# Recurrent mixer on TensorE: two dense pieces and then two recurrent steps, in place of one and one

## The chip, the cores and the metric

The kernel runs on one core of one Trainium2 chip. The metric is the device time of one execution in microseconds (us). TensorE is called PE, VectorE DVE, ScalarE ACT, GpSimd POOL, and SyncE SP.

## The reference, cut to what matters

A decoder block over 1024 tokens of width 1024. One large projection feeds two token mixers; what concerns the change is the recurrent one, with four heads of 128 keys and 128 values:

```python
proj = jnp.einsum('bsd,dn->bsn', h, w_in[i])
f = lb + (1.0 - lb) * jax.nn.sigmoid(f_lin)          # decay, per key and token
log_f, k, v, q = jnp.log(f), 1.0 - f, i_lin, jax.nn.silu(q_lin)
# S_t = diag(f_t) S_{t-1} + k_t v_t^T ;  o_t = S_t^T q_t, computed in chunks of tokens:
scores = jnp.einsum('bhtk,bhtsk,bhsk->bhts', q_c, decay, k_c)
o = einsum(scores, v_c) + einsum(q_c * exp(b), state)
new_state = exp(b_last) * state + einsum(k_c * exp(b_last - b), v_c)
o = o * lax.rsqrt(mean(o*o) + RMS_EPS) * norm_g * jax.nn.silu(og_lin)
```

Afterwards come a softmax mixer with eight heads, the merge of both, a squared-ReLU MLP, an embedding gate and two layer norms. The change touches none of these.

## The kernel before

**Dense work.** Weights are split into a high and a low part and each product is made of three matmul passes. A dense job is one 128-row block of the projection for all 1024 tokens. It has eight pieces, one for each 128 of the contraction; `feature_job` yields after each. A piece (`three_pass`, L774, L776, L778) is six matmuls of 128x512. A job writes one of two PSUM sets in turn, and before its first piece `begin` waits until the job before the last (same set) has been read, and until POOL has split its weights. At a job's end the semaphore `mm_done` lets ACT or DVE read it, and lets POOL convert (L683) and split (L686) the next weight chunk into the freed pages.

**Recurrent work.** Each head has 24 steps (`hg_step(n, i)`), which are called here:

- kt0, kt1 (i = 0, 1): transposes of the decayed keys, L864
- level 0 to level 15 (i = 2 to 17): two halves of the tokens at eight levels of the recursion over a 128-token chunk, 4 matmuls each, L882. Even levels are the first half of the tokens, odd ones the second.
- u0, u1 (i = 18, 19): state updates, L891
- o0, o1 (i = 20, 21): outputs, L901 and L904
- r0, r1 (i = 22, 23): means of squares, L909

These are plain float32 matmuls, and the profile records each as two. In each iteration of its own loop DVE forms the decay differences of a level (`level_sub`, L1721, L1722), multiplies those of the level before (`level_mul`, L1730, L1731) after ACT has taken their exponential (L1272), and merges the level before that by one more into the scores (`level_take`, L1737). Level i waits for the take of level i - 2 and for its own multiplications. Between them DVE has further work once in each head: `gate_part` (L1711) right behind take 0, L1781 behind take 2, `q_part` (L1681) behind take 6, `f_part` (L1686 to L1688) behind take 12, `decay_part` (L1695, L1701) behind take 14, and the states (L1748, L1750) and `kd_part` (L1706) behind take 15. u1 waits for take 15. At the end of a head ACT computes a logarithm (L1314) and an exponential (L1315) for r0 and then for r1, and DVE writes the head's output (`head_out`, L1761, L1762) for each before it begins the next head.

**The order on PE.** `dense_stream` gives 112 pieces of 14 jobs. Twelve pieces run first, then each recurrent step stands behind one piece (108 pieces, 96 steps), then four pieces are left. Jobs begin at pieces 0, 8, 16 and so on. In each head one job begins right behind level 1; it uses the PSUM set that `gate_part` must have read first. It is called the gated job here.

Of the kernel before, what the change touches and what calls it, by code (L numbers as in the profile page):

```python
# [27 lines left out]
NHG = 4  # L28
# [114 lines left out]
HG_LEAD = 12  # L143
# [67 lines left out]
def block_kernel(nc, x, p, ln0_g, ln0_b, w_in, hg_lb, hg_norm_g, fox_fb, w_a, w_b, w_o, ln1_g, ln1_b,  # L211
                 w_ff1, w_ff2, w_pg, w_p, ln2_g, ln2_b, c_ident, c_causal, c_masks,
                 h_scratch, c_scratch, pw_scratch, acc_scratch, act_scratch, out):
    with ExitStack() as ctx:
# [19 lines left out]
        def F(page, off=0, n=1024):  # L234
            t, at = f32_pages[page + off // 1024]
            return t[:, at + off % 1024:at + off % 1024 + n]
# [168 lines left out]
        def vtile(page, t):  # L405

            return F(page + t // 2, (t % 2) * HG, HG)
# [360 lines left out]
        def _(pe):  # L768
# [87 lines left out]
            def hg_step(n, i):  # L856
                par = n % 2
                if i < 2:

                    pe.wait_ge(kd_ready, n + 1)  # L860
                    if n:
                        pe.wait_ge(rs_ready, 2 * (n - 1) + i + 1)
                    for c in range(4 * i, 4 * i + 4):
                        ins = nc.tensor.transpose(bankM[i][:, (c % 4) * P:(c % 4 + 1) * P],  # L864
                                                  F(PG_T2, c * P, P), ident[:, :])
                    ins.then_inc(kt_turned, 1)
                elif i < 18:
                    hl = i - 2
                    lv, hf = hl // 2, hl % 2
                    if lv < LEVELS - 1:  # L870
                        pe.wait_ge(ab_ready, 14 * n + hl + 1)
                        base = PG_AB + (hl % 4) // 2
                        lhs = rhs = F(base, (hl % 2) * HALF, HALF)
                    else:
                        pe.wait_ge(q_ready, n + 1)
                        lhs, rhs = F(PG_HK + par, hf * HALF, HALF), F(PG_HQ + par, hf * HALF, HALF)
                    if lv == 0:
                        pe.wait_ge(kt_done, 2 * n + hf + 1)
                    else:
                        pe.wait_ge(pred_done, 16 * n + hl - 1)  # L880
                    for c in range(4):
                        ins = mm(bankM[hf][:, c * P:(c + 1) * P], lhs[:, c * P:(c + 1) * P],  # L882
                                 rhs[:, c * P:(c + 1) * P], start=True, stop=True)
                    ins.then_inc(lvl_done, 1)
                elif i < 20:
                    u = i - 18
                    pe.wait_ge(pred_done, 16 * n + 14 + u + 1)
                    pe.wait_ge(kt_done, 2 * n + u + 1)
                    pe.wait_ge(v_ready, TT)
                    for c in range(4 * u, min(4 * u + 4, TT - 1)):  # L890
                        ins = mm(bankM[u][:, (c % 4) * P:(c % 4 + 1) * P], F(PG_KT, c * P, P),  # L891
                                 vtile(PG_VHG, c)[:, n * P:(n + 1) * P], start=True, stop=True)
                    ins.then_inc(upd_done, 1)
                elif i < 22:
                    hf = i - 20
                    pe.wait_ge(st_ready, 2 * n + hf + 1)
                    pe.wait_ge(qe_ready, n + 1)
                    pe.wait_ge(pred_done, 16 * n + 16)
                    for c in range(4 * hf, 4 * hf + 4):
                        o = bankM[2 + hf][:, (c % 4) * P:(c % 4 + 1) * P]  # L900
                        ins = mm(o, vtile(PG_VHG, c)[:, n * P:(n + 1) * P], F(PG_S, c * P, P),  # L901
                                 start=True, stop=c == 0)
                        if c:
                            ins = mm(o, F(PG_ST, c * P, P), F(PG_T1, c * P, P), start=False, stop=True)  # L904
                    ins.then_inc(o_done, 1)
                else:
                    hf = i - 22
                    pe.wait_ge(sq_done, 2 * n + hf + 1)
                    mm(bankM[hf], mean_w[:, :], F(PG_T3, hf * HALF, HALF), start=True,  # L909
                       stop=True).then_inc(rms_done, 1)  # L910

            def dense_stream(names):
                for name in names:
                    yield from std(name)

            stream = dense_stream([("g", 0), ("q", 1), ("f", 1), ("g", 1), ("q", 2), ("f", 2), ("g", 2),
                                   ("q", 3), ("f", 3), ("g", 3), ("fq", 0), ("fk", 0), ("gx", 0), ("crow",)])
            for step in range(HG_LEAD + 24 * NHG):
                next(stream)
                if step >= HG_LEAD:  # L920
                    hg_step(*divmod(step - HG_LEAD, 24))
            for _ in stream:
                pass
            for t in range(TT):
# [43 lines left out]
            def turn_outputs(n):  # L968
                pe.wait_ge(o_ready, 16 * (n + 1))
                pe.wait_ge(x_ready, min(16 * (n + 1) + 2, 64))  # L970
                for i in range(TT):
# [4 lines left out]
            stream = dense_stream([(x, n) for n in range(1, NPAIR) for x in ("fq", "fk")]  # L976
                                  + [("gx", i) for i in range(1, 16)])
# [1216 lines left out]
```

## Time and profile before

| | |
|---|---|
| time, median of 3 runs | 1777.24 us (1775.79 to 1780.26) |
| time of the profiled execution | 1777.77 us |
| span of the profiled execution | 1775.8 us |
| PE busy | 1697.9 us, 96% of the span |
| DVE busy | 1028.1 us, 58% |
| mean granted clock of PE | 0.992 of full speed |
| recurrent mixer, first kt0 to last r1 | 117.3 to 352.4 us of the span |

Busy time is summed over the instructions of an engine. A wait is the idle time of an engine before an instruction, with the instruction that released it. "PEclk" is the granted clock of PE: 1.00 is 2.4 GHz and 0.50 is 1.2 GHz.

### The profile page before, as it was taken

The page shows a single profiled execution, that of the slowest core. Times are in us where ns is not written, and L with a number is a line of the kernel's source. Part 1 is how long each engine was busy: PE and PEld are TensorE (multiplying, and loading weights), DVE is VectorE, ACT ScalarE, POOL GpSimd, SP SyncE. Part 2 cuts the span into 40 slices and gives each one's busy share as a digit, 9 for nine tenths or more (in the row PEclk, how much of TensorE's full clock was granted, in tenths as well). Part 3 has the DMA queues.
Part 4 walks back from the last instruction along what each step waited for, and adds up shares of the span by engine and source line. Part 5 has one row for each costly group of instructions (what it writes and reads, how often), then busy time and mean ns, then how long its engine had stood idle before and what let it go on. Part 6 is the DMA issues. An engine that isn't in the chain of part 4 may idle for free.

```text
span 1775.8 us, 21568 instructions
## 1 busy us (share of the span) xinstructions
PE 1697.9 (96%) x8304; PEld 1381.6 (78%) x8304; DVE 1028.1 (58%) x1560; ACT 622.0 (35%) x954; POOL 623.6 (35%) x438
## 2 busy tenths in 40 slices
PE   4999999999999999999999998999999999999997
PEld 3888877886677678887878776788888887888886
DVE  7557987612222230003641676998766668866987
ACT  2143443213333333002012354244545453343341
POOL 3221121403011002333444438766665523342334
PEclk9999999999999999999999998999999999999999
DMA  8210000111001001111133343545443489778672
GB/s 275 71 48 25 24 25 25 47 48 48 25 25 48 25 12 37 48 48 36 52 103 109 129 155 108 174 150 209 163 163 131 148 275 306 227 224 238 196 228 95
DMA packets 207924, 200.80 MB, mean 113 GB/s; under 512 B 8520, under 2 KB 178760, under 8 KB 205776
## 3 DMA queue, kind: packets, MB, share of 16 engines
q1 hardware_dynamic: 204656, 188.35, 33.9%
q10 hardware_dynamic: 3168, 11.08, 1.6%
q8 instruction: 67, 1.10, 0.3%
q14 instruction: 33, 0.27, 0.1%
HBM read 153.23 MB, written 46.17 MB: 112 GB/s over the span
## 4 chain that ended last, share of the span: by engine, by line
PE 84%; DVE 9%; DMA 2%; SPq 2%; issue 1%; ACT 1%; POOL 1%; DVEq 0%; ACTq 0%; POOLq 0%
PE dense L774 10%; PE dense L776 10%; PE dense L778 10%; PE dense L964 3%; PE dense L1057 3%; PE dense L1059 3%; PE dense L1058 3%; PE dense L1137 3%; PE dense L1139 3%; PE dense L1138 3%; PE mixA L945 2%; PE mixA L943 2%; PE mixB L955 2%; PE dense L827 2%; PE dense L829 2%; PE dense L828 2%
## 5 line engine op out<-in xcount | busy, mean ns | idle before, releaser
L774 PE MATMUL dense<-parts 128*128 128x512 f32 x880 | 302.2, 413 | 7.5 <-DVE parts L1840 2.6
L683 POOL CAST parts<-page 128x1024 fp32r<-128x1024 f32 x55 | 61.3, 1114 | 681.9 <-PE dense L778 561.6
L776 PE MATMUL dense<-parts 128*128 128x512 f32 x880 | 284.9, 393 | 0.0
L778 PE MATMUL dense<-parts 128*128 128x512 f32 x880 | 283.8, 392 | 0.0
L686 POOL TENSOR_TENSOR parts<-page,parts 128x512 fp32r<-128x512 f32 x134 | 190.8, 1444 | 49.2 <-ACT parts L1406 44.8
L778 PEld LDWEIGHTS dense<-parts 128*128 128x128 f32 x880 | 166.1, 189 | 36.6
L776 PEld LDWEIGHTS dense<-parts 128*128 128x128 f32 x880 | 166.2, 189 | 35.7
L774 PEld LDWEIGHTS dense<-parts 128*128 128x128 f32 x880 | 154.6, 191 | 34.9 <-issue 9.2
L748 POOL TENSOR_TENSOR parts<-page,parts 128x512 fp32r<-128x512 f32 x52 | 89.8, 1749 | 208.8 <-ACT parts L1517 208.8
L1818 DVE CUSTOM_DVE_ANT_0 page<-mixA,page 128x128 f32<-128x128 f32 (+3 forms) x64 | 48.5, 758 | 190.0 <-PE mixA L946 190.0
L723 POOL TENSOR_TENSOR page<-page 128x512 f32<-128x512 f32 x80 | 123.1, 1538 | 59.4 <-PE dense L1059 26.4
L731 POOL TENSOR_TENSOR parts<-page,parts 128x512 fp32r<-128x512 f32 x80 | 113.4, 1419 | 61.7 <-ACT parts L1453 57.0
L1057 PE MATMUL dense<-parts 128*128 128x512 f32 x288 | 112.5, 391 | 0.3 <-issue 0.3
L1059 PE MATMUL dense<-parts 128*128 128x512 f32 x288 | 112.2, 390 | 0.0
L1058 PE MATMUL dense<-parts 128*128 128x512 f32 x288 | 112.1, 389 | 0.0
L1527 ACT CAST parts<-page 128x1024 fp32r<-128x1024 f32 x56 | 58.6, 1052 | 144.6 <-DVE page L2053 123.2
L1350 ACT ACTIVATE page<-page,nmx 128x128 f32<-128x128 f32 (+3 forms) x64 | 49.7, 777 | 166.0 <-DVE nmx L1823 166.0
L1453 ACT CAST parts<-page 128x512 fp32r<-128x512 f32 x132 | 78.2, 614 | 67.6 <-POOL page L723 62.7
L1840 DVE TENSOR_TENSOR parts<-page,parts 128x1024 fp32r<-128x1024 f32 x8 | 11.4, 1486 | 140.4 <-ACT parts L1366 140.4
L1137 PE MATMUL dense<-parts 128*128 128x512 f32 x224 | 87.4, 390 | 3.6 <-DVE parts L1978 3.6
L1138 PE MATMUL dense<-parts 128*128 128x512 f32 x224 | 87.2, 389 | 0.0
L1139 PE MATMUL dense<-parts 128*128 128x512 f32 x224 | 87.2, 389 | 0.0
(230 smaller groups left out, 3611.4 us busy)
## 6 DMA issues: line engine op xcount, KB each, us to landing
page<-in_w_ff SPq DMA_DIRECT2D x104, 512.0 KB, 5.9
page<-act_scratch SPq DMA_DIRECT2D x56, 512.0 KB, 5.8
page<-in_w_in SPq DMA_DIRECT2D x90, 256.0 KB, 3.4
act_scratch<-page SPq DMA_DIRECT2D x16, 1024.0 KB, 3.9
act_scratch<-page SPq DMA_DIRECT2D x16, 768.0 KB, 7.0
page<-in_w_o SPq DMA_DIRECT2D x32, 256.0 KB, 3.2
h_scratch<-page ACTq DMA_DIRECT2D x8, 512.0 KB, 2.8
page<-c_scratch SPq DMA_DIRECT2D x8, 512.0 KB, 4.2
```

What stands on the lines that cost most here:

```text
L686: ins = nc.gpsimd.tensor_tensor(R(lo, at, HALF), F(RAW + c % 2, at, HALF), R(hi, at, HALF).bitcast(F32), ALU.subtract)
L723: PT(raw(i), a, b, op).then_inc(s_sum, 1)
L731: PT(slot_half(q, i, True), F(SLOT[i], HALF, HALF), slot_half(q, i, False).bitcast(F32), ALU.subtract).then_inc(sum_split, 1)
L774: mm(o, whi, x_, start=first, stop=False)
L776: mm(o, whi, x_, start=False, stop=False)
L778: ins = mm(o, wlo, x_, start=False, stop=last)
L1057: mm(o, hi, x_part(i, k, False), start=k == 0, stop=False)
L1058: mm(o, hi, x_part(i, k, True), start=False, stop=False)
L1059: ins = mm(o, lo, x_part(i, k, False), start=False, stop=k == 3)
L1137: mm(o[:, cols], hi, xh, start=j == 0, stop=False)
L1138: mm(o[:, cols], hi, xl, start=False, stop=False)
L1139: ins = mm(o[:, cols], lo, xh, start=False, stop=j == 7)
```

## The change

The loop advances by two: two pieces are issued, then two steps. Odd steps keep their place among the pieces; each even step (kt0, the even levels, u0, o0, r0) goes behind one more piece and stands right before its odd neighbour. The count of pieces and steps is the same, and no other engine's program changes.

```diff
-            for step in range(HG_LEAD + 24 * NHG):
-                next(stream)
+            for step in range(0, HG_LEAD + 24 * NHG, 2):
+                for _ in range(2):
+                    next(stream)
                 if step >= HG_LEAD:
-                    hg_step(*divmod(step - HG_LEAD, 24))
+                    for s in (step, step + 1):
+                        hg_step(*divmod(s - HG_LEAD, 24))
```

## Rows read from the trace of the kernel before

**Rows 1.** Two windows: PE, PEld, DVE, ACT, POOL busy; PEclk, DMA, GB/s.
```profile
290.00:320.00 30.00, 26.54 (x143) 22.05 (x142) 27.92 (x53) 12.82 (x20) 8.86 (x6) 0.94 0.13 36
...
300.00:305.00 5.00, 4.99 (x23) 4.58 (x24) 5.00 (x13) 2.10 (x3) 0.71 (x1) 0.66 0.42 108
```
**Rows 2.** Waits in 98 to 362: us in total, times, longest.
```profile
PE mixA L882 <- DVE page L1737: 6.4, 8, 1.4
```
**Rows 3.** Timeline of PE (start, duration, line, shape, count): pieces and steps undisturbed.
```profile
109.10 0.61 PE L774 MATMUL dense<-parts 128*128 128x512 f32 x2
...
110.46 0.61 PE L774 MATMUL dense<-parts 128*128 128x512 f32 x2
...
195.07 1.05 PE L882 MATMUL mixA<-page 128*128 128x128 f32 x8
195.88 0.71 PE L774 MATMUL dense<-parts 128*128 128x512 f32 x2
...
197.35 1.05 PE L882 MATMUL mixA<-page 128*128 128x128 f32 x8
...
226.75 0.38 PE L901 MATMUL mixB<-page 128*128 128x128 f32 x2
...
228.46 0.70 PE L774 MATMUL dense<-parts 128*128 128x512 f32 x2
```
**Rows 4.** Timeline of PE: r1 of the first head; levels 0, 1 and gated job of the second.
```profile
173.30 1.02 PE L909 MATMUL mixA<-page,mean_w 128*128 128x512 f32 x2
...
179.41 1.16 PE L882 MATMUL mixA<-page 128*128 128x128 f32 x8
...
181.79 1.05 PE L882 MATMUL mixA<-page 128*128 128x128 f32 x8
183.94 0.70 PE L774 MATMUL dense<-parts 128*128 128x512 f32 x2 [1.10 <-DVE page L1711]
```
**Rows 5.** Timeline of DVE there: output for r1, first level_sub, take 0, gate.
```profile
175.75 0.69 DVE L1761 TENSOR_TENSOR page<-mixB,page 128x512 f32<-128x512 f32 x1 [0.31 <-ACT page L1315]
...
177.14 0.42 DVE L1721 TENSOR_TENSOR page<-page 128x256 f32<-128x256 f32 x1
...
181.96 0.73 DVE L1737 COPY_PREDICATED page<-masks,mixA 128x512 f32<-128x512 uint8 x1
182.58 1.21 DVE L1711 TENSOR_TENSOR page<-dense,page 128x1024 f32<-128x1024 f32 x1
```
**Rows 6.** Timeline of ACT there: logarithm and exponential for r1, and the next instruction.
```profile
174.36 0.69 ACT L1314 ACTIVATE page<-mixA,eps 128x512 f32<-128x512 f32 x1 [0.50 <-PE mixA L909]
175.08 0.63 ACT L1315 ACTIVATE page<-page 128x512 f32<-128x512 f32 x1
175.62 1.04 ACT L1226 ACTIVATE page<-page 128x1024 f32<-128x1024 f32 x1
```
**Rows 7.** Timelines of DVE (takes 14 and 15) and PE (u1), second head.
```profile
215.99 0.73 DVE L1737 COPY_PREDICATED page<-masks,mixA 128x512 f32<-128x512 uint8 x1 [1.03 <-PE mixA L882]
...
220.41 0.74 DVE L1737 COPY_PREDICATED page<-masks,mixA 128x512 f32<-128x512 uint8 x1
...
221.74 0.83 PE L891 MATMUL mixA<-page 128*128 128x128 f32 x6
```
**Rows 8.** First head: DVE's take 0 and a level_sub, POOL's split of a chunk.
```profile
122.01 0.73 DVE L1737 COPY_PREDICATED page<-masks,mixA 128x512 f32<-128x512 uint8 x1 [0.37 <-PE mixA L882]
...
124.72 1.50 DVE L1722 TENSOR_TENSOR page<-page 128x256 f32<-128x256 f32 x1
...
124.60 2.78 POOL L686 TENSOR_TENSOR parts<-page,parts 128x512 fp32r<-128x512 f32 x2
```
**Rows 9.** Timeline of POOL, fourth head: a chunk's conversion.
```profile
295.83 1.04 POOL L683 CAST parts<-page 128x1024 fp32r<-128x1024 f32 x1 [30.38 <-PE mixA L864]
```
**Rows 10.** Timeline of PE: two long stalls of the run.
```profile
300.01 2.08 PE L882 MATMUL mixA<-page 128*128 128x128 f32 x8 [2.91 <-DVE page L1731]
...
1065.62 1.06 PE L1030 MATMUL mixB<-ident,page 128*128 128x128 f32 x8 [2.52 <-issue]
```

## Prediction

> **What bounds the kernel now.** I read the page first. PE is the busy engine through nearly the whole span, as its table shows, so only PE's own work and PE's waiting count. Then the waits between 98 and 362 us, where the mixer runs: the largest of PE's is for DVE's takes, 6.4 us in 8 waits [rows 2]. The windows say why: from 290 to 320 PE was busy for 26.54 us of 30 and DVE for 27.92 [rows 1]. The reader is to see a balance of two engines. Last I read the timelines of PE, DVE, ACT and POOL over each head, since only the order of instructions changes, and no sum can show that. They show one pattern in each head: from its output work to take 11 DVE runs without a pause and PE waits for it; behind take 11 it is the other way round, and DVE waits for PE's levels.
>
> **The price of a switch.** The plain reason for such a change would be that PE loses time whenever it goes from one kind of matmul to the other. A piece alone takes 110.46 - 109.10 = 1.36 us. A level and a piece take 197.35 - 195.07 = 2.28, so a level standing alone costs 0.92. What does it cost right behind another step? Eight records run 195.88 - 195.07 = 0.81 us up to the next dense matmul, sixteen (o1) run 228.46 - 226.75 = 1.71: the eight more cost 0.90 [rows 3]. So a pair saves 0.02 us, and 48 pairs 1.0 us. From below the bound is nothing. From above it is the piece behind a step, 2.28 - 0.81 = 1.47 us against 1.36 alone: were all 0.11 us saved 48 times, that would be 5.3 us. I take 1.0, since a step gets 0.09 us back at its entry that a second one behind it can't get again.
>
> **What moves.** Odd steps stay where they are among the pieces, even ones come one piece, 1.36 us, later. The way from take i - 2 to level i keeps its two pieces and one step, and deadlines of even steps get later, which is harmless. What counts is what DVE or ACT begins when an even step is done and an odd step or a piece waits for. I went through a head with that question and found three places. At takes 2 to 10 the even level is still done before DVE comes to it (at take 6 by about 0.2 us, the least), and I cost them at nothing; if that cover is gone, a take starts some tenths later.
>
> Place one, level 0 to the gated job. Take 0 and the gate need 183.94 - 181.96 = 1.98 us up to the gated piece. In the second head level 0 now starts at about 180.57, at the end of two undisturbed pieces, and is done at 181.7; take 0 was at 181.96 anyway, as DVE was late [rows 4, 5]. So nothing is added, and the third head repeats this within 0.1 us. In the first head take 0 did wait for level 0, 0.37 us [rows 8], and now starts 1.36 us later, at 123.37.
>
> Place two, take 14 to u1. Take 14 waited 1.03 us for level 14; from its start to that of take 15, with the decay scans between, are 220.41 - 215.99 = 4.42 us. Level 14 comes 1.34 us later, take 15 starts near 221.75 and ends near 222.5, and u1, which started at 221.74, waits until about 222.65 [rows 7]. With some hundredths for a step behind a stall that is 0.95 us in each of the three heads that prepare a next one. The fourth has no decay work and loses nothing. Queued behind the waiting u1 are two pieces, o0, o1, two pieces, r0 and r1, so the whole next head is late by as much.
>
> Place three, r0 and r1. They now follow each other by 0.87 us in place of 2.24. ACT needs 0.72 us from r0's logarithm to its exponential and 0.54 from there to the next instruction. r1's logarithm started 174.36 - 173.30 = 1.06 us behind r1; now r0's starts at 0.17 and r1's at 1.43 [rows 4, 6]. DVE's output for r1 started 175.75 - 173.30 = 2.45 us behind r1 [rows 4, 5]; now that for r0 is only done at 2.96. So DVE starts the next head 0.5 us later, three times, and since it has no pause from there to take 11, PE gets this in full at level 11.
>
> **POOL against DVE.** A level_sub instruction of 0.42 us [rows 5] took 1.50 while POOL split a weight chunk, and POOL's two halves last 2.78 us [rows 8], so each such event costs DVE up to three caught instructions, about 0.6, 1.1 and 1.1 us. Takes and the gate keep their 0.73 and 1.21 us. A job's last piece now stands ahead of an even step, so POOL is set off about 0.9 us earlier. In the first head that is a gain: DVE waits for level 0 while POOL converts, take and gate cover the first half of the split, and one instruction is caught in place of three. With 1.36 for the late take 0 and 1.1 - 2.8 for the caught ones, take 1 comes 0.3 us earlier. In the second and third heads I take the meeting as before less 0.15 us, since POOL gets in when DVE reaches take 0. In the fourth a chunk moves from levels 1 to 3 to the time of the gate, which saves about 0.7.
> The Trainium skill (SBUF — State Buffer, Who interferes with whom) gives the reason: an instruction with two SBUF inputs and a GpSimd instruction that reads SBUF block each other for a whole instruction, and the order of issue decides which waits; one with at most one SBUF input stays out of it. The trace agrees, with 1.50 us for the one and 1.21 for the other. By the order of issue the meeting could also fall worse than I take it, which is rival B.
>
> **Sum without the clock.** First head: -0.3 at level 11, +0.95 for u1, +0.6. Second and third: 0.5 - 0.15 + 0.95 = +1.3 each. Fourth: 0.5 - 0.15 - 0.7 = -0.35, and -0.05 for a short wait that goes, -0.4. Together +2.8 us. The 1.0 us of the switches I don't subtract again: where DVE sets the pace it is worth nothing, and behind take 11 it is within the roundings of these positions.
>
> **The clock.** PE now issues two pieces and both levels ahead of the gated job and then has nothing. Its idle time there grows from 1.3 us to 2.2 in the second and third heads and comes to about 2.2 in the fourth, whose stall of 2.91 ahead of level 0 shrinks to about 1.5. Behind those 2.91 us eight records took 2.08 us for 1.05, behind 2.52 us they took 1.06 [rows 10]; the granted clock was 0.66 over 300 to 305 [rows 1], so part of it at the lower level of 1.2 GHz, and (1 - 0.66) x 5 = 1.7 us of work was lost. Of the six stalls of 1.8 to 2.9 us in the run before, three were followed by such a stretch. Behind the gated piece PE has only 0.3 us of slack to DVE, and DVE then waits for levels in turn, so I put 1.1 us of the 1.7 on the path. Half a chance at three places: +1.6 us, from 0 to 5.1. The sum is +4.4. It is made against an execution of 1777.77 us, 0.5 over the median of the runs; against the median of 1777.24 it gives 1781.6, and I say 1781.5.
>
> **The rivals.** A, no slower: switches cost what the piece behind a step shows, 0.11 us each, and PE's earlier positions pull DVE's along: 2.8 - 5.3 = -2.5 us, 1774.7; without the losses of places two and three it goes beyond -5.3. Against it speaks that DVE sets the pace up to take 11. Chance 0.15.
> B, slower: POOL, set off earlier, gets in among the level instructions before take 0, and holds them up by one or two caught ones, 1.1 to 2.2 us. The gate is late by that, PE's idle time ahead of the gated job goes to 3.3 us or more, and the low clock follows: 3 x (1.1 + 1.7) + 2.8 = +11.2 us, 1788.4, or some +7 where it happens once or twice. It decides from the point where POOL starts while DVE is between two SBUF instructions. For it: at 295.83 POOL did start so, and its conversion took the undisturbed 1.04 us [rows 9]. Against it: in its five other meetings with such a run of DVE it waited for a take. Chance 0.25.
> C, slower: a low clock behind every gated job but the first, in full: 2.8 + 3 x 1.7 = +7.9, 1785.1. Chance 0.15.
> D, my forecast: +2 to +5.3 us. Chance 0.45.
>
> **How the numbers follow.** What a measurement of this kernel can tell from no change is about 0.3%, 5.3 us. Faster beyond it is half of A, 0.07. Slower beyond it is most of B and C, 0.35. Within it are D, the other half of A and the mild ends of B and C, 0.58. The range of 1775.0 to 1788.0 leaves out the far ends of A and B, at most 0.15; D's own is 1779.0 to 1782.5.
>
> **What would show it.** In the changed profile: u1 with a wait of about 0.9 us for a take in the first three heads; a wait for the gate ahead of L774 in all four, 1.2 us in the first and 2 in the others; r1's logarithm on ACT without idle time before it; take 0 of the first head at 123.4. PEclk under 1.00 behind the gated jobs is the clock's part. I am wrong if POOL catches DVE before take 0, if DVE has to wait for the even levels 2 to 10, or if the pieces themselves change their pace by more than 0.02 us for a pair.

## The result, and the profile after

The changed kernel takes 1796.18 us (median of 4 runs, 1794.63 to 1797.33) against 1776.56 us for the kernel before in the same session: ratio 1.0107, 95% interval 1.0091 to 1.0123. It is slower by 19.6 us where I had forecast slower by 4. Its profiled span is 1795.0 us against 1775.8.

The page's busy times, and PE's waits between 98 and 380 us (us in total, times, longest):

```profile
PE 1704.2 (95%) x8304; PEld 1387.8 (77%) x8304; DVE 1024.1 (57%) x1560; ACT 622.9 (35%) x954; POOL 619.0 (34%) x438
```
```profile
PE dense L774 <- DVE page L1713: 10.9, 4, 4.2
...
PE mixA L882 <- DVE page L1733: 5.9, 4, 4.2
PE mixA L882 <- DVE page L1739: 5.4, 7, 0.8
```

The waits for takes have become smaller, 5.4 us against 6.4 [rows 2]. In their place stand 10.9 us of waits for `gate_part` (L1713), the longest 4.2 us; the kernel before had 2.2 us of them on this list, in two waits. Two windows, in the second and third heads (PE, PEld, DVE, ACT, POOL busy; PEclk) add the clock:

```profile
170.00:200.00 30.00, 25.20 (x123) 20.65 (x122) 20.14 (x39) 15.13 (x22) 3.80 (x3) 0.89 0.10 27
230.00:260.00 30.00, 25.23 (x126) 20.70 (x127) 19.00 (x37) 14.54 (x21) 7.43 (x6) 0.89 0.13 36
```

Where in the mixer the time went is read from one checkpoint, the first L774 behind r1 of each head. It stood at 173.75, 232.62, 291.49 and 352.38 us before, and stands at 174.88, 240.93, 306.39 and 370.02 now. So the four heads cost +1.13, +7.18, +6.59 and +2.74, together +17.6 of the span's +19.2 us. The other 1.6 lie outside the mixer, and I haven't followed them.

The second head on PE, then on POOL, DVE and ACT:

```profile
173.56 1.88 PE L909 MATMUL mixA<-page,mean_w 128*128 128x512 f32 x4
...
181.66 1.05 PE L882 MATMUL mixA<-page 128*128 128x128 f32 x8
183.37 1.16 PE L882 MATMUL mixA<-page 128*128 128x128 f32 x8 [0.65 <-DVE page L1733]
188.67 1.19 PE L774 MATMUL dense<-parts 128*128 128x512 f32 x2 [4.15 <-DVE page L1713]
...
191.37 1.05 PE L774 MATMUL dense<-parts 128*128 128x512 f32 x2
...
193.93 2.37 PE L882 MATMUL mixA<-page 128*128 128x128 f32 x16
...
229.95 0.94 PE L891 MATMUL mixA<-page 128*128 128x128 f32 x6 [0.72 <-DVE page L1739]
```
```profile
181.96 1.07 POOL L683 CAST parts<-page 128x1024 fp32r<-128x1024 f32 x1 [14.27 <-PE dense L778]
183.11 2.72 POOL L686 TENSOR_TENSOR parts<-page,parts 128x512 fp32r<-128x512 f32 x2
```
```profile
181.72 0.42 DVE L1732 TENSOR_TENSOR page<-page 128x256 f32<-128x256 f32 x1
182.06 1.25 DVE L1733 TENSOR_TENSOR page<-page 128x256 f32<-128x256 f32 x1
183.23 1.49 DVE L1723 TENSOR_TENSOR page<-page 128x256 f32<-128x256 f32 x1
184.64 1.48 DVE L1724 TENSOR_TENSOR page<-page 128x256 f32<-128x256 f32 x1
...
186.71 0.71 DVE L1739 COPY_PREDICATED page<-masks,mixA 128x512 f32<-128x512 uint8 x1
187.32 1.20 DVE L1713 TENSOR_TENSOR page<-dense,page 128x1024 f32<-128x1024 f32 x1
...
189.79 0.72 DVE L1739 COPY_PREDICATED page<-masks,mixA 128x512 f32<-128x512 uint8 x1
...
195.45 0.73 DVE L1739 COPY_PREDICATED page<-masks,mixA 128x512 f32<-128x512 uint8 x1 [3.63 <-PE mixA L882]
```
```profile
174.68 0.69 ACT L1316 ACTIVATE page<-mixA,eps 128x512 f32<-128x512 f32 x1 [1.08 <-PE mixA L909]
...
175.93 0.67 ACT L1316 ACTIVATE page<-mixA,eps 128x512 f32<-128x512 f32 x1
```

The reader is to see this. POOL's conversion starts at 181.96, while DVE is between `level_mul` instructions and 4.75 us ahead of take 0 (186.71). Three DVE instructions of 0.42 us then take 1.25, 1.49 and 1.48. Take 0 and the gate come late, PE stands idle for 4.15 us, and the two pieces behind that run at 1.05 us for two records in place of 0.61. They take 193.93 - 188.67 = 5.26 us, while two pieces together took 2 x 1.36 = 2.7 undisturbed [rows 3]. DVE has used up its lead and waits 3.63 us for level 2.

In the kernel before, the corresponding conversion started at 182.09, just behind the start of take 0 (181.96 [rows 5]). It had not been waiting for that take: the piece that releases it ended only then, at 181.33 + 0.62 = 181.95. The end of that piece, the conversion, and DVE's rows of that kernel behind take 0, with takes 1 and 2:

```profile
181.33 0.62 PE L778 MATMUL dense<-parts 128*128 128x512 f32 x2
```
```profile
182.09 1.04 POOL L683 CAST parts<-page 128x1024 fp32r<-128x1024 f32 x1 [14.42 <-PE dense L778]
```
```profile
183.71 1.05 DVE L1721 TENSOR_TENSOR page<-page 128x256 f32<-128x256 f32 x1
184.68 1.51 DVE L1722 TENSOR_TENSOR page<-page 128x256 f32<-128x256 f32 x1
...
186.78 0.73 DVE L1737 COPY_PREDICATED page<-masks,mixA 128x512 f32<-128x512 uint8 x1
188.74 0.73 DVE L1737 COPY_PREDICATED page<-masks,mixA 128x512 f32<-128x512 uint8 x1
```

With the starts of the takes counted from the checkpoint of the head before, the second head can be laid side by side (us; the last two kernels are experiments below):

| | take 0 | take 1 | take 2 | take 9 | take 11 | next checkpoint |
|---|---|---|---|---|---|---|
| before | 8.21 | 13.03 | 14.99 | 33.37 | 36.62 | 58.87 |
| changed | 11.83 | 14.91 | 20.57 | 39.68 | 42.91 | 66.05 |
| changed, POOL held to take 0 | 8.85 | 14.16 | 16.34 | 35.41 | 38.65 | 61.77 |
| before, POOL held to take 11 | 8.20 | 11.28 | 13.24 | 29.17 | 33.25 | 58.05 |

Read across: +3.62 at take 0, +1.88 at take 1 (in the kernel before two instructions were caught behind the gate), +5.58 at take 2 (the slow pieces), +6.3 at takes 9 and 11, and +7.18 at the end, with u1's wait.

### The profile page after: what moved, and what is told of

Same layout as the page of the kernel before. It is cut to its first block, busy times and chain, and to the rows that moved or that the text cites. A ratio compares the mean times of both kernels' runs of the same rounds, so it can differ in the third digit from the quotient of the medians.

```text
span 1795.0 us, 21568 instructions
## 1 busy us (share of the span) xinstructions
PE 1704.2 (95%) x8304; PEld 1387.8 (77%) x8304; DVE 1024.1 (57%) x1560; ACT 622.9 (35%) x954; POOL 619.0 (34%) x438
## 4 chain that ended last, share of the span: by engine, by line
PE 84%; DVE 10%; DMA 2%; issue 1%; ACT 1%; SPq 1%; POOL 1%; DVEq 0%; ACTq 0%; POOLq 0%
PE dense L774 10%; PE dense L776 10%; PE dense L778 10%; PE dense L966 3%; PE dense L1059 3%; PE dense L1060 3%; PE dense L1061 3%; PE dense L1139 3%; PE dense L1140 3%; PE dense L1141 3%; PE mixA L947 2%; PE mixA L945 2%; PE mixB L957 2%; PE dense L829 2%; PE dense L828 2%; PE dense L827 2%
## 5 line engine op out<-in xcount | busy, mean ns | idle before, releaser
L774 PE MATMUL dense<-parts 128*128 128x512 f32 x880 | 297.9, 408 | 16.2 <-DVE page L1713 10.9
L778 PEld LDWEIGHTS dense<-parts 128*128 128x128 f32 x880 | 167.0, 190 | 36.6
L776 PEld LDWEIGHTS dense<-parts 128*128 128x128 f32 x880 | 167.0, 190 | 35.9
L774 PEld LDWEIGHTS dense<-parts 128*128 128x128 f32 x880 | 158.4, 191 | 46.2 <-issue 16.3
L1842 DVE TENSOR_TENSOR parts<-page,parts 128x1024 fp32r<-128x1024 f32 x8 | 11.4, 1488 | 140.4 <-ACT parts L1368 140.4
```

The costliest lines, as they stand in the source:

```text
L774: mm(o, whi, x_, start=first, stop=False)
L776: mm(o, whi, x_, start=False, stop=False)
L778: ins = mm(o, wlo, x_, start=False, stop=last)
```

## The experiments

The theory that I took from this trace was rival B: POOL gets in before take 0, the gate is late, the low clock follows. Its rivals were that the other pairs carry the loss, that the wait and not POOL causes it, and that a switch between kinds of matmuls has a price after all. Each kernel was timed against the kernel before in its own session, where the median of that was 1777.0 to 1777.2 us. "Heads" are the lengths of heads two, three and four between checkpoints: 58.87, 58.87, 60.89 before.

**One pair at a time.** The loop of the kernel before, with only the named steps issued as a pair behind two pieces:

```diff
+            PAIRED = (2,)
...
+                elif i in PAIRED:
+                    next(stream)
+                    hg_step(*divmod(step - HG_LEAD, 24))
+                    hg_step(*divmod(step + 1 - HG_LEAD, 24))
```

Levels 0 and 1 alone, `PAIRED = (2,)`:

> The kernel before, with only levels 0 and 1 of each head paired (two pieces, level 0, level 1). Theory P (POOL meets DVE early): the last piece of a job now ends ahead of level 0, POOL starts its conversion about 0.9 to 1.2 us earlier and catches three level instructions before take 0 in the second and third heads; the gated job starts about 3 us later there, the low clock follows, and the time rises by 9 us or more. Rival G (the gate is late only because level 0 is late): 1.3 us in the first head and nothing in the others, so +1 us in all.

r0 and r1 alone, `PAIRED = (22,)`:

> The kernel before, with only r0 and r1 of each head paired. Theory: ACT handles r1 0.4 us later and DVE's output for r1 starts 0.5 to 0.65 us later, in three heads: +1.6 to +2 us. If the delay of DVE alone lets POOL's conversion (which stays where it was) land among the level instructions before take 0, one is caught, the gate is another 0.8 us late, and it is +4 us or, with the low clock, more. Rival: the delay is absorbed before take 0 and nothing changes.

Levels 14 and 15 alone, `PAIRED = (16,)`:

> The kernel before, with only levels 14 and 15 of each head paired. Theory: take 14 starts 1.3 us later, take 15 behind the decay work too, and the state update u1 waits 0.7 to 0.95 us for it in three heads: +2.5 us. Rival: the wait is hidden behind something else and the time stays within 1 us.

Levels 2 to 13, `PAIRED = (4, 6, 8, 10, 12, 14)`:

> The kernel before, with the levels 2 to 13 paired and nothing else: 24 pairs. Theory: a pair saves 0.02 us and no wait is added, so 0 to -1 us, with POOL's second meeting in each head moved from before take 9 to before take 8, at the same cost. Rival S (a switch costs PE the 0.11 us that the piece behind a step shows): -2.6 us.

| paired | us | ratio, 95% interval | heads |
|---|---|---|---|
| levels 0, 1 | 1778.25 | 1.0008 (0.9999 to 1.0016) | 58.62, 58.67, 64.37 |
| r0, r1 | 1777.55 | 1.0005 (0.9996 to 1.0014) | 59.48, 59.43, 61.85 |
| levels 14, 15 | 1779.81 | 1.0015 (1.0007 to 1.0023) | 59.78, 59.72, 61.80 |
| levels 2 to 13 | 1779.01 | 1.0008 (1.0000 to 1.0017) | 59.32, 60.90, 61.00 |

The pair of levels 14 and 15 costs 0.9 us in heads two and three, with a wait of 0.7 us at u1 (place two, forecast 0.95). The fourth head, where I had forecast nothing, lengthens by 0.9 too, by another way: a level waits 0.89 us there for a take that POOL's conversion at 325.40 has delayed. r0 and r1 cost 0.6 in heads two and three (place three) and 1.0 in the fourth. Levels 2 to 13 bring nothing with 24 pairs; had each saved 0.11 us, it would be -2.6, so rival A falls. They cost 0.5 in the second head, all of it ahead of take 9 (33.89 in place of 33.37), and POOL's second conversion falls one take earlier there. The third head loses 1.6 us more, behind take 11: the granted clock is 0.72 from 268 to 273 us, behind two waits for takes of only 0.91 and 0.82 us. The pairs kt, u and o I haven't tried alone. And the pair that I held to be the cause costs heads two and three nothing. POOL and DVE in its second head:

```profile
180.69 2.07 POOL L683 CAST parts<-page 128x1024 fp32r<-128x1024 f32 x1 [13.20 <-PE dense L778]
```
```profile
181.11 0.41 DVE L1740 TENSOR_TENSOR page<-page 128x256 f32<-128x256 f32 x1
181.45 0.42 DVE L1741 TENSOR_TENSOR page<-page 128x256 f32<-128x256 f32 x1
181.78 0.73 DVE L1747 COPY_PREDICATED page<-masks,mixA 128x512 f32<-128x512 uint8 x1
```

The conversion is requested 1.1 us ahead of take 0 and takes 2.07 us in place of 1.04: it waited until take 0 ran, and DVE lost nothing ahead of the take. That an earlier request is enough for POOL to get in is refuted for these two heads. In the fourth head it is enough: 64.37 us in place of 60.89.

**Two pairs together**, `PAIRED = (2, 22)`:

> The kernel before, with levels 0 and 1 and r0 and r1 of each head paired; alone they cost 1.4 and 0.9 us. Theory P2 (it takes both: the early end of the job's last piece, and DVE 0.6 us later, so that POOL's conversion arrives between the two multiplications before take 0 and gets in): the second and third heads lengthen by 3.5 to 7 us each as in the changed kernel, 8 to 14 us in all, about 1787. Rival: the costs add up, +2.5 us, and the changed kernel's loss has another source.

1786.35 us, ratio 1.0046 (1.0034 to 1.0059), heads 61.71, 61.79, 64.73. The two pairs add 1.4 and 0.9 us alone by their ratios and 8 together. The rows are those of the changed kernel again:

```profile
179.97 1.05 POOL L683 CAST parts<-page 128x1024 fp32r<-128x1024 f32 x1 [13.19 <-PE dense L778]
```
```profile
180.04 1.26 DVE L1741 TENSOR_TENSOR page<-page 128x256 f32<-128x256 f32 x1
181.22 1.49 DVE L1731 TENSOR_TENSOR page<-page 128x256 f32<-128x256 f32 x1
182.63 1.48 DVE L1732 TENSOR_TENSOR page<-page 128x256 f32<-128x256 f32 x1
...
184.70 0.71 DVE L1747 COPY_PREDICATED page<-masks,mixA 128x512 f32<-128x512 uint8 x1
```
```profile
186.66 1.19 PE L774 MATMUL dense<-parts 128*128 128x512 f32 x2 [4.15 <-DVE page L1721]
...
189.36 1.39 PE L882 MATMUL mixA<-page 128*128 128x128 f32 x8
```

The late gate is the same too, but the head is 2.8 us longer than before and not 7.2. Behind the gate the clock is low again (0.66 from 185 to 190 us), yet for one piece only, since level 2 is not paired here and stands right behind it. Take 2 comes 2.9 us later than in the kernel before (17.93), in the changed kernel 5.6. The same wait and low clock cost little where the level that DVE needs is not behind two slow pieces.

**The changed kernel less one of the two pairs.**

The loop above with one of these two lines, the first without the pair of levels 0 and 1, the second without r0 and r1:

```diff
+            PAIRED = (0, 4, 6, 8, 10, 12, 14, 16, 18, 20, 22)
+            PAIRED = (0, 2, 4, 6, 8, 10, 12, 14, 16, 18, 20)
```

> The changed kernel with levels 0 and 1 of each head unpaired again. By P2 the conversion starts behind take 0 and the gate comes in time: what is left are places two and three, 0.9 + 0.6 us in three heads, and some tenths from the levels: 1781 to 1784, 12 to 15 us less than the changed kernel. Rival: the pairs of the other levels carry a good part of the loss, and it stays above 1788.

> The changed kernel with r0 and r1 of each head unpaired again. By P2 DVE is not late, POOL's conversion arrives at the moment at which it lost to DVE in the kernel with levels 0 and 1 paired, and the gate is late only in the fourth head: 1781 to 1786. Rival (pairing levels 0 and 1 is enough together with the other levels): 1790 or more.

Without the pair of levels 0 and 1: 1784.35 us, 1.0041 (1.0028 to 1.0055), heads 60.92, 60.92, 62.30. Without r0 and r1: 1784.03, 1.0035 (1.0023 to 1.0048), heads 60.03, 60.05, 64.84. Either way some 12 us of the 19 are gone, since in heads two and three POOL gets in ahead of take 0 only with both of them. The second head adds up without an interaction here: r, levels 14/15 and levels 2 to 13 give 0.6 + 0.9 + 0.45 = 1.95 (measured 2.05), and with -0.25 for levels 0/1 in place of r 1.1 (measured 1.2). The third heads measure the same (2.05 and 1.2), so the stretch of low clock that levels 2 to 13 alone had there is not in them.

**POOL held back in the changed kernel until take 0** (four conversions, one in each head):

```diff
+                    if c in (11, 14, 17, 20):
+                        pool.wait_ge(pred_done, 16 * ((c - 11) // 3) + 1)
```

> The changed kernel, with POOL's conversion of the chunk behind the gated job's predecessor (chunks 11, 14, 17, 20) held back until take 0 of the head. Theory P: the gate is no longer behind caught instructions, the wait for it falls from 4.2 to about 2.2 us in the second and third heads, the caught instructions come behind the gate as in the kernel before, and the low clock is rarer: 5 to 9 us less than the changed kernel, so about 1788 to 1791. Rival G (pairing levels 0 and 1 makes the gate late by itself): within 1 us of the changed kernel.

1784.79 us, 1.0046 (1.0033 to 1.0059), so 11.4 us below the changed kernel with every pair in place: of its loss of 19.6 us against the kernel before, 7.6 are left. Heads 61.77, 61.76, 62.48. The gated job of the second head now waits 2.01 us:

```profile
186.24 0.72 PE L776 MATMUL dense<-parts 128*128 128x512 f32 x2 [2.01 <-DVE page L1723]
```

That is the 2 us that the forecast had for the gate. From 180 to 200 us the granted clock is still only 0.91, so part of that stretch is at 1.2 GHz.

**PE kept busy while it waits.** Sixteen matmuls of 128x512 into a PSUM bank that nobody reads then, behind level 1 of heads two and three:

```diff
+                if step >= HG_LEAD and i == 2 and step // 24 in (1, 2):
+                    pe.wait_ge(y_done, 2 * ((step - HG_LEAD) // 24))
+                    for _ in range(16):
+                        mm(mixB[:, 0:HALF], R(XHI, 0, P), R(XHI, 0, HALF), start=True, stop=True)
```

> The changed kernel, with 16 extra matmuls of 128x512 into a PSUM half that nobody reads then, behind level 1 of the second and third heads, while PE would wait for the gate (extra work, whose result is overwritten). They take 3.4 us of the 4.2 us wait. Theory C (the low clock behind the long wait costs 2.8 us in each of these heads): the granted clock stays 1.00 there and the time falls by 4 to 6 us, though more work is done. Rival: what was lost behind the gated job was DVE's lateness and not the clock; the time stays.

1792.16 us, 1.0084 (1.0070 to 1.0098). The two filled heads take 63.21 and 63.24 us against 66.05 and 65.46: -2.8 and -2.2, although PE does more. The windows of this kernel:

```profile
180.00:240.00 60.00, 56.43 (x328) 48.11 (x327) 47.64 (x92) 23.40 (x32) 13.10 (x9) 1.00 0.10 27
240.00:300.00 60.00, 56.48 (x334) 48.47 (x331) 48.62 (x96) 21.95 (x32) 7.89 (x6) 1.00 0.07 18
```

In the changed kernel both read 0.94. The late gate is the same here (take 0 at 11.88, take 1 at 14.96), and take 2 stands at 17.78 in place of 20.57, so these 2.2 to 2.8 us a head are the clock's. The window from 300 to 360 us, with the unfilled fourth head, has 0.91.

**POOL held back until take 11**, in the kernel before and in the changed one. Behind take 11 DVE waits for PE anyway:

```diff
+                    if 11 <= c <= 21 and c not in (13, 16):
+                        pool.wait_ge(pred_done, 16 * min((c - 11) // 3, 3) + 12)
```

In the branch of chunk 19, `pool.wait_ge(pred_done, 16 * 3 + 12)` is added.

> The kernel before, with POOL's conversions of chunks 11, 12, 14, 15, 17, 18, 19, 20, 21 held back until take 11 of their head, where DVE has spare time. If POOL's meetings with DVE set the pace of the kernel before too, PE's waits for takes 3 and 9, for the gate and for level 0 of the fourth head shrink or go: -6 to -11 us against the kernel before. Rival: DVE's own work sets the pace and only some tenths for each head come back, -1 us.

> The changed kernel with the same conversions held back until take 11. Theory: what is left of the change's loss are the three places of the prediction, 1.3 (take 0 of the first head and its like) to 6 us over the kernel before with the same hold; so 1772 to 1776, at least 18 us under the changed kernel. Rival: a loss of over 10 us against the held kernel before would mean that pairing costs by itself what is put down to POOL.

The kernel before with it takes 1767.99 us, ratio 0.9947 (0.9933 to 0.9960), heads 58.05, 58.09, 56.72: 9 us faster than before and the fastest of all. Its waits on these lines between 98 and 380 us:

```profile
PE mixA L894 <- DVE page L1740: 3.3, 3, 1.1
PE dense L777 <- DVE page L1714: 3.2, 3, 1.1
```

No wait of a level for a take is among its largest, and the granted clock is 1.00 through the mixer. The changed kernel with it takes 1774.65 us, 0.9985 (0.9976 to 0.9993), heads 59.04, 60.60, 57.05: 21.5 us below the changed kernel, and 6.7 above the kernel before held in the same way. Of these 21.5 us some 9 are what the hold brings without the change, so the comparison that counts is 6.7 against 19.6: about 13 us of the change's loss, two thirds, go with POOL's place. What is left is about the size of places one to three and one stretch of low clock. PE waits 2.0 us for the gate in the second, third and fourth head alike, but only in the third does the clock fall behind it (1.00 from 180 to 186 us, 0.83 from 240 to 246), and that head is 1.6 us longer than the second.

**The moment of the request.** Levels 0 and 1 paired as in the first experiment, with the conversions of heads two and three held back within DVE's run, to 0.43 us ahead of take 0 in place of 1.09, to see whether the moment within DVE's instructions decides who gets in:

```diff
+                    if c in (14, 17):
+                        pool.wait_ge(ab_sub, 14 * ((c - 11) // 3) + 4)
```

> The kernel with only levels 0 and 1 paired, and POOL's conversion in the second and third heads held until DVE has done the level_sub of level 3, so 0.5 us later than it came by itself, when it lost to DVE until take 0. Theory P3 (the moment of arrival alone decides whether POOL gets in among the level instructions): it gets in, takes 1.0 to 1.3 us, and three instructions are caught before take 0; +2 to +3 us for each of the two heads at the gate, more with the low clock: 1782 to 1788. Rival: a request made inside DVE's run always waits for the take, and the time is that of the kernel with levels 0 and 1 paired.

1777.92 us, 1.0006 (0.9997 to 1.0015), heads 58.69, 58.62, 65.38:

```profile
179.94 1.41 POOL L685 CAST parts<-page 128x1024 fp32r<-128x1024 f32 x1 [13.85 <-DVE page L1734]
```
```profile
179.70 0.42 DVE L1742 TENSOR_TENSOR page<-page 128x256 f32<-128x256 f32 x1
180.03 0.42 DVE L1743 TENSOR_TENSOR page<-page 128x256 f32<-128x256 f32 x1
180.37 0.73 DVE L1749 COPY_PREDICATED page<-masks,mixA 128x512 f32<-128x512 uint8 x1
```

POOL lost. It began 0.24 us behind the start of a DVE instruction, just as it did in the changed kernel (181.96 against 181.72), where it won. The moment as the trace shows it doesn't decide.

## Why the prediction was wrong

**The step that failed** is "In the second and third heads I take the meeting as before less 0.15 us, since POOL gets in when DVE reaches take 0". I had read the waiting for a take as a rule and the one exception [rows 9] as chance, and gave rival B 0.25. In the changed kernel POOL gets in 4.75 us ahead of take 0 of head two, likewise in head three (248.04, take 0 at 252.77), and the gate is late by 3.6 us. It takes the earlier request (levels 0, 1) and the later DVE (r0, r1) together. I had costed both edits, and each alone as harmless to the meeting, which is right in these two heads; the combination I took from the single ones. I had also not asked why the meeting fell on take 0 before. Level 0 waits for DVE's multiplication, one piece stood behind level 0, and the end of that piece released POOL, so POOL followed DVE: with only r0 and r1 paired, level 0 waits 0.69 us for DVE and the conversion still starts 0.13 us behind take 0 (181.85 and 181.72). Pairing levels 0 and 1 puts that piece ahead of level 0 and cuts this tie.

**The second head, term by term** (from the table of takes):

| | predicted | measured |
|---|---|---|
| place three, r0 and r1 | +0.5 | +0.64 (take 0 held, 8.85 - 8.21) |
| meeting of DVE and POOL up to take 1 | -0.15 | +1.24 (1.88 - 0.64) |
| from take 1 to take 2: late gate, and clock | +1.1 at half a chance | +3.7 (5.58 - 1.88), of it 2.8 the clock by the filled kernel |
| the next chunk's meeting, up to take 9 | 0 | +0.7 (6.31 - 5.58) |
| place two, u1 | +0.95 | +0.9 (7.18 - 6.29) |
| sum | +1.3, and 0.55 for the clock | +7.2 |

The net cost of the meeting itself is small; dear is that it falls ahead of the gate. DVE gets half of the 3.6 us back by take 1, but PE stands idle for 4.15 us and then runs slowly.

**The clock.** That a low clock follows a long wait at the gate was right, the size was off twice: I had expected a wait of 2 us and half a chance of 1.1 us on the path. The wait was 4.15, the stretch behind it came in both heads, and cost 2.8 and 2.2. Behind 2.01 us it came too, in the held kernel, but takes 1 and 2 are 2.18 us apart there against 1.96 before, so it cost hardly anything. Behind 2.02 us, with POOL held until take 11, it came in one of three heads, and behind waits under 1 us in one head with levels 2 to 13 paired: the length of the wait alone doesn't decide it.

**The fourth head.** Forecast -0.4, measured +2.74. I had expected the moved chunk to meet the gate, where it costs nothing. POOL converts and splits two chunks in one go and catches six instructions ahead of take 0; level 0 waits 4.17 us, against 2.91 before [rows 10], and runs at the low clock:

```profile
317.51 1.94 PE L882 MATMUL mixA<-page 128*128 128x128 f32 x8 [4.17 <-DVE page L1733]
```

It goes with the pair of levels 0 and 1: heads four of 64.37, 64.73, 64.84 and 65.38 us in the experiments that pair them and only part of the rest (63.63 in the changed kernel), at most 62.30 in those that don't.

**Right** were the first head up to take 1 and, roughly, the prices that need no meeting. The first head's rows:

```profile
123.50 0.74 DVE L1739 COPY_PREDICATED page<-masks,mixA 128x512 f32<-128x512 uint8 x1 [0.84 <-PE mixA L882]
124.13 1.21 DVE L1713 TENSOR_TENSOR page<-dense,page 128x1024 f32<-128x1024 f32 x1
125.26 1.37 DVE L1723 TENSOR_TENSOR page<-page 128x256 f32<-128x256 f32 x1
...
127.55 0.73 DVE L1739 COPY_PREDICATED page<-masks,mixA 128x512 f32<-128x512 uint8 x1
```

Take 0 at 123.5 (forecast 123.37), one caught instruction in place of three, take 1 earlier than before. The head costs +1.13 (forecast +0.6). u1 has its wait, 0.72 us where I had 0.9, and ACT's second logarithm no idle time before it. A switch between kinds of matmuls costs next to nothing. Two pieces and two levels, undisturbed in the changed kernel, take 207.95 - 203.43 = 4.52 us, and before 2 x 2.28 = 4.56 [rows 3]: a pair saves 0.04 us, where I had 0.02.

```profile
203.43 1.95 PE L882 MATMUL mixA<-page 128*128 128x128 f32 x16
...
207.95 1.95 PE L882 MATMUL mixA<-page 128*128 128x128 f32 x16
```

**What stays open** is who gets in when POOL's conversion meets a run of DVE instructions with two SBUF inputs. The outcome is the same in heads two and three of each of these kernels, but neither the moment of the request nor its distance from the take explains it. The clearest case is in the first head, where the conversion starts 0.01 us behind the first instruction that follows take 7. In the changed kernel it got in behind that instruction and took 1.30 us; in the same kernel without the pair of r0 and r1 it waited through four instructions until take 8 and took 2.32:

```profile
142.19 1.30 POOL L683 CAST parts<-page 128x1024 fp32r<-128x1024 f32 x1 [15.84 <-PE dense L778]
```
```profile
142.22 2.32 POOL L683 CAST parts<-page 128x1024 fp32r<-128x1024 f32 x1 [15.83 <-PE dense L778]
```

The Trainium skill (SBUF — State Buffer, Who interferes with whom) says that the port pair which VectorE shares with GpSimd is an exclusive lock, and that the order of issue decides who is blocked. The trace agrees that a caught instruction waits for a whole one (1.49 us for 0.42). But if the one that asks first came first, POOL would have had to get in behind one DVE instruction in every case, and the conversion of 2.07 us has waited through about three.

## What to carry to other kernels

An order on one engine also sets when it releases the others. Go through each engine that the moved work sets off and ask what it meets there; where the meeting has shown two outcomes, price both, and don't add up single edits. A wait of 4 us on TensorE cost up to 2.8 us more than its length, by the low clock behind it, and next to nothing more where only one slow piece stood ahead of the step that VectorE needed. Work of GpSimd that nobody is waiting for belongs where VectorE idles: holding it until take 11 was worth 9 us, and the change that was tried under it cost 6.7 in place of 19.

## What the runs showed of the hardware

- A POOL conversion that meets a run of DVE instructions with two SBUF inputs can wait through several of them, up to the take, which reads PSUM: 2.07 us in two kernels, 1.41 in one, 2.33 and 2.39 in the kernel before, for an undisturbed 1.04. It doesn't always: the one at 142.19 took 1.30 and got in behind the first. If it gets in at once, its conversion and split (1.04 + 2.7 us) catch three, by 0.83, 1.07 and 1.06 us.
- The granted clock fell behind waits of 4.15 and of 2.01 us, behind one of three waits of 2.01 to 2.02 us in another kernel, and once behind two waits of 0.91 and 0.82 us. Sixteen matmuls put into the wait of 4.15 us kept it at 1.00.
